# The input projections xr, gr, q and k of a two-layer float32 block, computed with weight columns as the stationary tile

## What is computed

```python
xn = rmsnorm(h, norm_mix_g[l])
u = jnp.einsum('bsd,de->bse', xn, w_in[l])
q, k, v, xr, gr, ga, gb = jnp.split(u, splits, axis=-1)       # 1024 columns each
ya = chunked_band_attention(q, k, v, rel_table[l]) @ w_attn_out[l]
xc = causal_depthwise_conv(xr, conv_w[l], conv_b[l])          # 4 taps along the tokens
hr = rg_lru(xc, w_rg_r[l], b_rg_r[l], w_rg_i[l], b_rg_i[l], rg_lambda[l])
yb = (hr * jax.nn.gelu(gr)) @ w_rnn_out[l]
gates = jax.nn.sigmoid(jnp.concatenate([ga, gb], axis=-1) + b_merge[l])
h = h + (g_a * ya + g_b * yb) @ w_o[l]
```

## Time and profile before

| | us |
|---|---|
| median of 3 runs | 998.67 (997.17 to 1002.05) |
| the profiled execution, its own time | 994.14 |
| its span, first to last instruction | 992.4 |
| PE busy | 952.9 |
| DVE busy | 502.7 |
| ACT busy | 491.2 |
| POOL busy | 337.3 |

### The profile page before, as it was taken

The page is one execution under the profiler, slowest core; times in us unless marked ns, Lnnn a source line. Parts: engine busy times, 40 slices in busy tenths (PEclk is TensorE's granted clock), DMA queues, the critical chain, the costliest instruction groups (busy, mean ns, idle before and its releaser), DMA issues.

```text
span 992.4 us, 13886 instructions
## 1 busy us (share of the span) xinstructions
PE 952.9 (96%) x4548; PEld 786.9 (79%) x4548; DVE 502.7 (51%) x841; ACT 491.2 (49%) x771; POOL 337.3 (34%) x170
## 2 busy tenths in 40 slices
PE   8998979999999999999999999998999989999997
PEld 6876867888878888888878888887878868888886
DVE  5439596554544434343564434337488674334332
ACT  5353935654455454444544454436436464444442
POOL 2410000102434444344444444553512034343442
PEclk9999999999999999999999999999999999999999
DMA  7844454354655566778566566655612246665562
GB/s 232 282 131 147 144 173 141 109 153 142 204 161 181 174 190 190 239 225 242 175 183 190 171 192 188 188 157 161 190 43 86 85 147 194 192 187 175 190 190 81
DMA packets 132768, 169.29 MB, mean 171 GB/s; under 512 B 16707, under 2 KB 88430, under 8 KB 132598
## 3 DMA queue, kind: packets, MB, share of 16 engines
q1 hardware_dynamic: 132566, 168.67, 55.1%
q10 hardware_dynamic: 160, 0.07, 0.0%
HBM read 167.61 MB, written 1.10 MB: 170 GB/s over the span
## 4 chain that ended last, share of the span: by engine, by line
PE 79%; DVE 11%; ACT 5%; issue 3%; DMA 0%; POOL 0%; DVEq 0%; POOLq 0%; ACTq 0%; SPq 0%
PE acc L786 24%; PE acc L788 24%; PE acc L787 24%; PE tp L831 4%; DVE w_lo L1173 4%; ACT w_hi L462 1%; PE sc L916 1%; PE acc L1108 1%; DVE u L1261 1%; ACT junk L468 1%; DVE xt_lo L1556 1%; DVE u L1225 0%; DVE u L1321 0%; DVE h L1546 0%; PE tp L936 0%
## 5 line engine op out<-in xcount | busy, mean ns | idle before, releaser
L462 ACT ACTIVATE w_hi<-w_raw 128x1024 fp32r<-128x1024 f32 x305 | 322.0, 1060 | 376.2 <-PE acc L788 346.0
L1770 POOL TENSOR_TENSOR w_lo<-w_raw,w_hi 128x1024 fp32r<-128x1024 f32 x124 | 302.5, 2440 | 397.0 <-ACT w_hi L462 396.9
L1173 DVE TENSOR_TENSOR w_lo<-w_raw,w_hi 128x1024 fp32r<-128x1024 f32 x181 | 234.8, 1306 | 330.6 <-ACT w_hi L462 328.9
L786 PE MATMUL acc<-w_hi,xt_hi 128*128 128x512 f32 (+1 forms) x880 | 350.0, 398 | 9.5 <-DVE w_lo L1173 6.6
L788 PE MATMUL acc<-w_lo,xt_hi 128*128 128x512 f32 (+1 forms) x880 | 342.9, 390 | 0.0
L787 PE MATMUL acc<-w_hi,xt_lo 128*128 128x512 f32 (+1 forms) x880 | 342.2, 389 | 0.0
L786 PEld LDWEIGHTS acc<-w_hi,xt_hi 128*128 128x128 f32 x880 | 165.3, 188 | 46.6 <-DVE w_lo L1173 9.7
L788 PEld LDWEIGHTS acc<-w_lo,xt_hi 128*128 128x128 f32 x880 | 165.1, 188 | 34.7
L787 PEld LDWEIGHTS acc<-w_hi,xt_lo 128*128 128x128 f32 x880 | 165.5, 188 | 32.0
L786 PE MATMUL acc<-w_hi,hid_hi 128*128 128x512 f32 x264 | 103.2, 391 | 0.0
L788 PE MATMUL acc<-w_lo,hid_hi 128*128 128x512 f32 x264 | 102.8, 389 | 0.0
(11 more groups left out here) (198 smaller groups left out, 781.7 us busy)
## 6 DMA issues: line engine op xcount, KB each, us to landing
w_raw<-in_ffn_w_gu SPq DMA_DIRECT2D x176, 256.0 KB
w_raw<-in_w_in SPq DMA_DIRECT2D x68, 512.0 KB
w_raw<-in_w_ffn_in SPq DMA_DIRECT2D x88, 256.0 KB
w_raw<-in_ffn_w_down SPq DMA_DIRECT2D x44, 512.0 KB
w_raw<-in_w_ffn_out SPq DMA_DIRECT2D x22, 512.0 KB
w_raw<-in_w_rnn_out SPq DMA_DIRECT2D x8, 512.0 KB
w_raw<-in_w_attn_out SPq DMA_DIRECT2D x8, 512.0 KB
w_raw<-in_w_o SPq DMA_DIRECT2D x8, 512.0 KB
```

The costliest lines, as they stand in the source:

```text
L462: act.activation(w_hi[:, b, :], w_raw[:, b, :], ACT.Copy).then_inc(hi_done[b], 1)
L786: pe.matmul(o, hi[:, k, rows], wh, start=first and n == 0, stop=False)
L1173: dve.tensor_tensor(w_lo[:, b, :], w_raw[:, b, :], w_hi[:, b, :].bitcast(F32), ALU.subtract).then_inc(lo_done[b], 1)
L1770: pool.tensor_tensor(w_lo[:, b, :], w_raw[:, b, :], w_hi[:, b, :].bitcast(F32), ALU.subtract).then_inc(lo_done[b], 1)
```

## The change

xr, gr, q and k (groups 0 to 7) are computed turned: a tile of 128 x 128 of the weight is stationary and 256 columns of x transposed stream, so a slab has 24 matmuls of 256 columns in place of 12 of 512, and the result has features on the partitions. The scale rs then lies along the free dimension: DVE spreads it to columns (`rs_cols`), PE turns it once, and DVE keeps it as a row `rx_row`, plain and times 1/8 for q. `evict_turned` multiplies with that row and writes straight to `xrT`, `grT` and `qkT`. The turns of xr, gr, q and k and their copies are gone; gelu works in place on ACT. The parameter turn moves from behind slab 16 to behind slab 4. The convolution moves to slabs 8 to 13 in DVE's queue, the gates to two tiles behind each of slabs 12 to 15 in PE's, with slabs 16 to 19 fed between tanh on ACT. SP loads the block-diagonal weights before slab 8 instead of after slab 15. POOL's queue has the same low halves. The diff, with semaphores and unchanged lines left out:

```diff
-X = starts([("x", 4), ("par", 1), ("xg", 8), ("gate", 8), ("qk", 8), ("p1", 16), ("at", 4), ("mt", 4), ("h1", 4),
+X = starts([("x", 4), ("rs", 1), ("par", 1), ("gate", 8), ("p1", 16), ("at", 4), ("mt", 4), ("h1", 4),
...
+    rs_cols = pt1[:, 1, 0:T].rearrange("p (m t) -> p m t", m=MT)
+    rx_row = sb1[:, :, 0:T]
...
-    rows_k(w_in, 4, 3, 3 * D + W)
+    rows_k(w_in, 4, 1, 3 * D + W)
...
+    with sp.Fori(0, 2) as c:
+        for q in range(4):
+            slab(8 + q, rect(8 + q, w_in, 256 * q, c * W + 4 * D), c, 1)
...
-    with act.Fori(0, 2) as i:
-        feed(4, 8, i, 2)
-    act.wait_ge(set_up, 2)
-    for n in range(4):
-        x = X["xg"] + 2 * n
-        wait_tp_full(act, x)
-        act.activation(xrT[:, 2 * n:2 * n + 2, 3:3 + T],
-                       two(tp[x % 2]), ACT.Copy).then_inc(tp_free[x % 2], 1)
-        x += 1
-        wait_tp_full(act, x)
-        act.activation(grT[:, 2 * n:2 * n + 2, :], two(tp[x % 2]),
-                       ACT.Gelu_apprx_tanh).then_inc(tp_free[x % 2], 1)
+    feed(4, 6)
...
-    feed(20, 11)
+    feed(10, 6)
+    def gelu(g):
+        for b in range(2):
+            wait_drained(act, g, b)
+            v = grT[:, 4 * (g - 2) + 2 * b:4 * (g - 2) + 2 * b + 2, :]
+            act.activation(v, v, ACT.Gelu_apprx_tanh).then_inc(gelu_done, 1)
+    gelu(2)
...
+        if n % 2 == 0:
+            feed(16 + n // 2, 1)
...
+    gelu(3)
...
+        if n % 2 == 0:
+            feed(20 + n // 2, 1)
...
-        if n % 2 and n < 7:
-            feed(31 + n // 2, 1)
-    feed(34, 1)
-    feed(35, 1)
+    feed(24, 4)
...
-    feed(36, 2)
-    for n in range(4):
-        x = X["qk"] + 2 * n
-        wait_tp_full(act, x)
-        act.activation(qkT[:, 2 * n:2 * n + 2, :], two(tp[x % 2]),
-                       ACT.Copy, scale=HD ** -0.5).then_inc(tp_free[x % 2], 1)
-        feed((38, 39, 41, 42)[n], (1, 2, 1, 1)[n])
+    feed(28, 8)
...
-    feed(43, 1)
+    feed(36, 8)
...
+    def group_turned(s, g, ready=None, after={}):
+        banks = acc[g % 2 * 2:g % 2 * 2 + 2]
+        for q in range(4):
+            r = (s + q) % RING
+            pe.wait_ge(lo_done[r], (s + q) // RING + 1)
+            if ready is not None:
+                ready(q)
+            if q == 0:
+                wait_bank(pe, g, 1)
+            for b in range(2):
+                for c in (2 * b, 2 * b + 1):
+                    for j in range(2):
+                        k, cols = 2 * q + j, slice(j * W + c * P, j * W + (c + 1) * P)
+                        o = banks[b][:, c % 2 * T:(c % 2 + 1) * T]
+                        pe.matmul(o, w_hi[:, r, cols], xt_hi[:, k, :], start=q == 0 and c == 2 * b and j == 0,
+                                  stop=False, skip_group_check=True)
+                        pe.matmul(o, w_hi[:, r, cols], xt_lo[:, k, :], start=False, stop=False,
+                                  skip_group_check=True)
+                        mm = pe.matmul(o, w_lo[:, r, cols], xt_hi[:, k, :], start=False, stop=q == 3 and j == 1,
+                                       skip_group_check=True)
+                if b == 0 and q == 3:
+                    mm.then_inc(acc0_full[g % 2], 1)
+                if b == 1:
+                    mm.then_inc(slab_used[r], 1)
+            if q in after:
+                after[q]()
...
-    group(0, 0, XT, 4, ready=pairs_ready(X["x"]), after={0: lambda: turn_x(2), 1: lambda: turn_x(3)})
-    for g in range(1, 4):
-        group(4 * g, g, XT, 4)
-    def turn_xr_gr(tile_pairs):
-        for g in range(4):
-            wait_both_drained(pe, g)
-        for n in tile_pairs:
-            turn_tiles(X["xg"] + 2 * n, u[:, 0], (2 * n, 2 * n + 1))
-            turn_tiles(X["xg"] + 2 * n + 1, u[:, 1], (2 * n, 2 * n + 1))
-    def turn_parameters():
+    def turn_rs_and_parameters():
+        pe.wait_ge(rs_spread, 1)
+        turn(X["rs"], [(m * P, rs_cols[:, m, :]) for m in range(MT)])
...
-        turn_xr_gr((0, 1))
-    group(16, 4, XT, 4, after={0: turn_parameters, 1: lambda: turn_xr_gr((2, 3))})
-    group(20, 5, XT, 4)
-    def gates():
+    def gates(n0):
...
-        for n in range(KT):
+        for n in (n0, n0 + 1):
...
-    def turn_q_k(n):
-        for sec in (2, 3):
-            wait_both_drained(pe, 2 * sec + n // 2)
-            turn_tiles(X["qk"] + 2 * n + sec - 2, u[:, sec], (2 * n, 2 * n + 1))
-    group(24, 6, XT, 4, after={2: gates})
-    group(28, 7, XT, 4)
-    group(32, 8, XT, 4, after={1: lambda: turn_q_k(0), 2: lambda: turn_q_k(1)})
-    group(36, 9, XT, 4, after={0: lambda: turn_q_k(2), 1: lambda: turn_q_k(3)})
-    wait_tp_free(pe, X["qk"] + 6)
-    wait_tp_free(pe, X["qk"] + 7)
+    group_turned(0, 0, ready=pairs_ready(X["x"]), after={0: lambda: turn_x(2), 1: lambda: turn_x(3)})
+    group_turned(4, 1, after={0: turn_rs_and_parameters})
+    group_turned(8, 2)
+    group_turned(12, 3, after={q: lambda q=q: gates(2 * q) for q in range(4)})
+    for g in range(4, 8):
+        group_turned(4 * g, g)
+    group(32, 8, XT, 4)
+    group(36, 9, XT, 4)
+    wait_both_drained(pe, 6)
+    wait_both_drained(pe, 7)
...
-    with dve.Fori(0, 2) as i:
-        for g in range(2):
-            feed(4 + 4 * g, 4, i, 2)
-            drain_scaled(g, lambda m: u[:, bass.ds(i, 1), m, g * W:(g + 1) * W].rearrange("p a n -> p (a n)"),
-                         i, 2, 1, 4 * g + 3, rx)
+    dve.tensor_copy(rs_cols, rx.unsqueeze(2).to_broadcast([P, MT, P])).then_inc(rs_spread, 1)
+    feed(4, 4)
+    wait_tp_full(dve, X["rs"])
+    step(dve.tensor_copy(rx_row[:, 0, :], tp[X["rs"] % 2][:, 0:T]))
+    dve.tensor_scalar(rx_row[:, 1, :], tp[X["rs"] % 2][:, 0:T], HD ** -0.5, None,
+                      ALU.mult).then_inc(tp_free[X["rs"] % 2], 1)
...
+    def evict_turned(g, dst, row=0):
+        for b in range(2):
+            wait_acc(dve, g, b, 4 * g + 3)
+            tiles = slice(4 * (g % 2) + 2 * b, 4 * (g % 2) + 2 * b + 2)
+            dve.tensor_tensor(dst(tiles), two(acc[g % 2 * 2 + b]),
+                              rx_row[:, row, :].unsqueeze(1).to_broadcast([P, 2, T]),
+                              ALU.mult).then_inc(acc_drained[g % 2 * 2 + b], 1)
+    def to_xr(tiles):
+        return xrT[:, tiles, 3:3 + T]
+    wait_tp_free(dve, X["rs"])
+    evict_turned(0, to_xr)
...
-    wait_tp_free(dve, X["xg"] + 6)
-    wait_tp_free(dve, X["xg"] + 7)
...
-    feed(20, 2)
+    wait_both_drained(dve, 0)
...
-    feed(22, 2)
+    feed(8, 2)
...
-    drain_section(4)
-    feed(24, 2)
+    evict_turned(1, to_xr)
+    feed(10, 2)
+    wait_both_drained(dve, 1)
+    conv_tiles((4, 5))
+    feed(12, 2)
+    conv_tiles((6, 7))
...
-    conv_tiles((4, 5))
-    feed(26, 2)
-    conv_tiles((6, 7))
-    drain_section(5)
-    dve.wait_ge(table_landed, 16)
-    dve.tensor_copy(ext_sb[:, 256:384], ext_sb[:, 255:256].to_broadcast([HEADS, P])).then_inc(ext_done, 1)
-    feed(28, 4)
-    drain_section(6)
-    feed(32, 2)
+    evict_turned(2, lambda tiles: grT[:, tiles, :])
+    feed(14, 4)
+    evict_turned(3, lambda tiles: grT[:, tiles, :])
+    feed(18, 4)
+    wait_tp_free(dve, X["gate"] + 6)
+    wait_tp_free(dve, X["gate"] + 7)
+    dve.wait_ge(conv_done, KT)
+    step(dve.scalar_tensor_tensor(ti[:], ti[:], 1.0, xcT, ALU.add, ALU.mult))
+    feed(22, 1)
+    evict_turned(4, lambda tiles: qkT[:, tiles, :], 1)
+    feed(23, 2)
...
+    feed(25, 1)
...
-    feed(34, 2)
-    wait_tp_free(dve, X["gate"] + 6)
-    wait_tp_free(dve, X["gate"] + 7)
-    step(dve.scalar_tensor_tensor(ti[:], ti[:], 1.0, xcT, ALU.add, ALU.mult))
-    drain_section(7)
-    def copy_k(n):
-        x = X["qk"] + 2 * n + 1
-        wait_tp_full(dve, x)
-        dve.tensor_copy(qkT[:, KT + 2 * n:KT + 2 * n + 2, :], two(tp[x % 2])).then_inc(tp_free[x % 2], 1)
+    feed(26, 1)
+    evict_turned(5, lambda tiles: qkT[:, tiles, :], 1)
+    feed(27, 2)
+    dve.wait_ge(table_landed, 16)
+    dve.tensor_copy(ext_sb[:, 256:384], ext_sb[:, 255:256].to_broadcast([HEADS, P])).then_inc(ext_done, 1)
+    dve.wait_ge(mult_done, 1)
+    dve.scalar_tensor_tensor(ti[:], ti[:], 0.5, sq, ALU.mult, ALU.mult).then_inc(bx_done, 1)
+    feed(29, 1)
...
-    feed(36, 2)
-    copy_k(0)
-    dve.wait_ge(mult_done, 1)
-    dve.scalar_tensor_tensor(ti[:], ti[:], 0.5, sq, ALU.mult, ALU.mult).then_inc(bx_done, 1)
...
-    feed(38, 2)
-    copy_k(1)
+    feed(30, 1)
+    def to_k(tiles):
+        return qkT[:, slice(KT + tiles.start, KT + tiles.stop), :]
+    evict_turned(6, to_k)
...
-    drain_section(8)
-    feed(40, 2)
-    copy_k(2)
-    copy_k(3)
+    feed(31, 2)
...
+    dve.wait_ge(gelu_done, 4)
...
-    feed(42, 2)
-    drain_section(9)
+    feed(33, 2)
+    evict_turned(7, to_k)
+    feed(35, 2)
...
+    def drain_section(g):
+        drain_scaled(g, lambda m: u[:, g // 2, m, g % 2 * W:(g % 2 + 1) * W], last_slab=4 * g + 3, scale=rx)
+    feed(37, 2)
+    drain_section(8)
+    feed(39, 4)
+    drain_section(9)
+    feed(43, 1)
...
-    with pool.Fori(0, 2) as i:
-        feed(4, 8, i, 2)
+    feed(4, 16)
...
-    wait_tp_free(pool, X["qk"])
```

(7 more changed lines are left out.)

## The result

The changed kernel takes 985.1 us (median of 4 runs, 983.9 to 987.3) beside 998.9 for the kernel before (median of 4 runs, 997.2 to 1002.1): a ratio of 0.9866, 95% interval 0.9847 to 0.9885. It is faster by 13.8 us. The forecast was 992.5, 6.2 us faster: right in sign and inside its range, but 7.4 us above what was measured. The profiled execution has a time of 987.3 and a span of 985.5 us at a mean granted clock of 0.994.

What follows compares the result with a forecast made beforehand. PE's queue was taken as the bound (busy 96% of the span). First scores 3.8 us earlier plus 2.4 from the first attention round made 6.2 us, so 998.7 became 992.5; range 982 to 1001 over all cases.

Steps and rivals of the forecast that it cites:

- the time of the first scores: Start of the first attention scores on PE: 145.1 us instead of 148.9, 3.8 us of the gain.
- the DVE chain: DVE's queue from 26.2 us through convolution, polynomial and group 2's eviction: through at 60.1, with 9.2 us for POOL meetings.
- ACT between the eviction and the third gate tile: ACT's gelu 0.6, high half 1.06, table load 1.28 and tanh 0.9 us: third gate tile starts about 64.0.
- the last of the sum: Final step: median 998.7, 4.5 above the profiled execution, and the same 6.2 us off gives 992.5.
- Clock, before: PE's waits in the kernel before, the longest half of 6 us: granted clock stays at 1.00, 2.4 GHz, through all.
- Turned slabs: PE, 24 matmuls of 256 columns per slab, 0.1192 us each with hidden weight loads: 2.86 us, 0.13 more than now.
- Rival 2: PE's turned slabs: weight loads aren't hidden; gate-pass spacing of 0.22 us would add 42 us, giving 1035; chance 0.06.
- Rival 4: Supply of slabs, not PE, sets the pace; 10 us of waits come back elsewhere: no change, 998; chance 0.06.
- rival 1: DVE and POOL don't get in each other's way: scores at 134.0, 17.3 us less, 981.4; chance 0.18.
- Clock, after: PE after its new 6 us idle before the third gate tile: clock may fall to 1.2 GHz, costing 1.9 us.
- rival 3: Clock stays low between PE's stops from 64 to 76 us: +9.6 over the forecast, 1002; chance 0.10.
- First round: First attention round, 20.58 us: PE's wait for the first softmax goes as yt_lo moves earlier, 2.4 us less.

Runs made afterwards that it cites:

- a_again: The changed kernel run once more with no edit, beside the kernel before: median 986.1 us (6 runs), ratio 0.9879.
- b_again: The kernel before, run once more with no edit: median 997.8 us (12 runs), ratio 1.0006; its profiled execution took 997.75 us.
- b_split: The kernel before with matmuls of slabs 0 to 31 cut in two of 256 columns, x still stationary: 1001.35 us, ratio 1.0031.
- a_lo_dve: The changed kernel with the low halves of slabs 9 to 19 that POOL made now made by DVE: 980.2 us, ratio 0.9818.
- a_fill: The changed kernel with nine unused matmuls filling PE's idle before the third gate tile: 984.2 us, ratio 0.9857.
- a_yt_late: The changed kernel with yt_lo put back behind the low half of slab 43, just ahead of the first maxima: 986.5 us, ratio 0.9883.

## Why the prediction was right and wrong, point by point

**Two steps failed.** The first is the time of the first scores. The sum has them at 145.1; a_again, with an ordinary start, has them at 141.6, 3.5 us earlier. Three terms on the way were too large, by 1.5 us (the DVE chain), 1.5 (ACT between the eviction and the third gate tile) and 1.0 (the gates), and the slabs were 0.4 too small; the points below take them one by one.

The second is the last of the sum: "the median of the runs shown is 998.7, 4.5 above the profiled one, and the same 6.2 off gives 992.5". It takes the 4.5 us for something that both kernels share. b_again shows what such a difference is made of, falls of the clock after waits of PE, 1.6 us of them at the very wait that the change removes. a_again has 1.6 us of such falls, the one at 264 us, besides the one that the sum counts for itself. So 2.9 of the 4.5 us were too much.

Both together close the sum for a_again: 992.5 - 3.5 - 2.9 = 986.1, as measured. The first result, 985.1, lies 1.0 lower; the intervals of the two ratios overlap, and no run says more about that. From the sum's own base the forecast was 987.9, and the profiled execution after took 987.3; that agreement is luck. Its scores came 2.1 us early (3.5, less 1.4 for a late transfer of x and a fall of the clock behind it), and a fall at 268 us that the sum didn't have took 1.6 back.

Between two executions that have their falls, b_again and a_again, the gain is 7.3 us up to the first scores (148.89 to 141.61), 2.4 in the first round and 1.6 for the fall at the softmax wait; then b_again loses 2.0 us to two more falls and a_again 1.6 to one. That is all of the 11.7 us between them. The forecast had 3.8, 2.4 and 0.

**Clock, before.** "through all those the granted clock stays at 1.00" held for one execution and was read as a property of the kernel. That it stood 4.5 us under the median was the hint that it wasn't.

**Turned slabs: right.** The timeline of PE and of weight loads in the kernel after, inside a turned slab (compare):

```profile
99.70 0.28 PE L840 MATMUL acc<-xt_lo,w_hi 128*128 128x256 f32 x1
99.82 0.28 PE L842 MATMUL acc<-xt_hi,w_lo 128*128 128x256 f32 x1
...
99.70 0.19 PEld L842 LDWEIGHTS acc<-xt_hi,w_lo 128*128 128x128 f32 x1
99.82 0.19 PEld L838 LDWEIGHTS acc<-xt_hi,w_hi 128*128 128x128 f32 x1
```

Starts are 0.12 us apart with a load of 0.19 us for each: 24 matmuls in 2.86 to 2.87 us, and 24 slabs in 68.05 us for 67.6 forecast. Rival 2 is out, and b_split prices the form by itself. The Trainium skill (TensorE: Matmul & The Clock Gate, "What overlaps and what doesn't") lets a weight load overlap a running matmul only in another row group; in this trace both use all 128 rows and overlap throughout, so the measurement decides against it here. Rival 4 is out as well: no gap before slabs 16 to 39.

**The DVE chain: right in kind, 1.5 us too long.** Forecast from 26.2 to 60.1, 33.9 us; measured 27.6 to 60.0, 32.4. The four meetings cost 2.07, 2.17, 2.07 and 2.15 us (the groups above less their times in a_lo_dve), 8.5 together for 9.2; the five small operations took 0.5 us for 0.9. `consts_ready` came at 58.8, as forecast, from a start that was 1.4 us late. The first pair of convolution tiles met nothing: it was POOL that waited there. POOL in the kernel after:

```profile
32.58 4.29 POOL L1802 TENSOR_TENSOR w_lo<-w_raw,w_hi 128x1024 fp32r<-128x1024 f32 x1 [2.71 <-ACT w_hi L469]
37.64 2.40 POOL L1802 TENSOR_TENSOR w_lo<-w_raw,w_hi 128x1024 fp32r<-128x1024 f32 x1 [0.76 <-ACT w_hi L469]
...
51.53 4.20 POOL L1802 TENSOR_TENSOR w_lo<-w_raw,w_hi 128x1024 fp32r<-128x1024 f32 x1 [5.04 <-ACT w_hi L469]
```

4.29 us for an operation that takes 2.40. So slab 8 was not late (1.5 forecast), slab 10 came 2.3 us late and slab 12 0.4. Two turned evictions took 1.28 us for 1.33, undisturbed in the middle of POOL's work. As a forecast for the change rival 1 is refuted by the chain above. That its 981.4 lay nearer to the result than 992.5 comes from the steps named at the start, of which 0.7 us at most have to do with POOL (8.5 for 9.2). a_lo_dve builds the case without meetings: its first scores are at 134.86, near the rival's 134.0, though 6.8 us before a_again's and not the 11.1 that the rival put between its own and the forecast's.

**ACT before the gates: one term was not there.** ACT in the kernel after:

```profile
51.47 1.28 ACT L512 ACT_TABLE_LOAD   x1
59.45 1.23 ACT L512 ACTIVATE grT<-grT 128x512 f32<-128x512 f32 x2 [6.69 <-DVE grT L1255]
60.58 1.04 ACT L469 ACTIVATE w_hi<-w_raw 128x1024 fp32r<-128x1024 f32 x1
61.53 0.46 ACT L521 ACTIVATE u<-tp,small 128x256 f32<-128x256 f32 x1
...
79.34 1.28 ACT L532 ACT_TABLE_LOAD   x1
```

The load stands ahead of gelu, in ACT's idle time, and none stands between gelu and tanh. The forecast had put 1.28 us between them, the duration of the earlier trace rows, where a load stands before another operation. Without it, 2.5 us passed from the eviction to the third gate tile for 4.0. The tile came at 62.49 instead of 64.1, and the idle was 4.2 us for 6.

**Clock, after: right in kind.** After the idle the first gate passes of the kernel after run long:

```profile
63.57 1.06 PE L903 MATMUL tp<-u,blockdiag 128*128 128x256 f32 x2
64.42 1.06 PE L904 MATMUL tp<-u,blockdiag 128*128 128x256 f32 x2
64.92 0.78 PE L838 MATMUL acc<-xt_hi,w_hi 128*128 128x256 f32 x1
65.49 0.41 PE L840 MATMUL acc<-xt_lo,w_hi 128*128 128x256 f32 x1
65.70 0.41 PE L842 MATMUL acc<-xt_hi,w_lo 128*128 128x256 f32 x1
```

Matmuls of 256 columns start 0.21 us apart, the 1.2 GHz level again, for 0.12. It cost 1.7 us (a_fill) for 1.9 forecast. It didn't stay low between stops, so rival 3 is out. What the forecast lacked is that shorter waits do the same: at 266.96, after 1.91 us behind DVE (L1455), the next matmuls of 512 columns are 0.43 apart too, 1.6 us.

**Gates with slabs 14 and 15**: 10.7 us without the fall for 11.5, so the restarts were priced 0.8 too high. **First round**: 18.19 us, 2.4 less, as forecast, and the maxima start 2.5 us behind the scores for 2.6. `yt_lo` is not all of it (a_yt_late). **Start**: slab 4 at 24.3 for 22.7 in the profiled execution and 22.9 in a_again, so the forecast stands and the first trace had a late transfer of x. In sum for the first scores: start +1.4, chain -1.5, ACT -1.5, gates -1.0, slabs +0.4 make 142.9 out of 145.1; measured 142.97. In a_again the start is 0, and the same terms make 141.5; measured 141.61.

## What to carry to other kernels

Price an edit against an execution that looks like the median: where the profiled one lies several us under it, its waits are cheaper than usual, and a wait of 2 us that goes may take as much again in clock with it. When operations move on DVE, look at what POOL runs at that time; here four meetings of 2.1 us each were worth more than sharing the low halves with POOL, and moving them off POOL, with one activation put behind the ones that PE waits for, gave 8 to 9 us more than the change alone.

## What the runs showed of the hardware that was not expected

- A DVE operation with a single tensor operand, SBUF to SBUF, is held by POOL's as well: 53.43 us, 128x8 elements, 2.33 us instead of 0.18. The Trainium skill (GPSIMD Engine Reference, "Key points") names two SBUF inputs or a 2-port mode as the condition; no run here shows which mode this one was in. Evictions out of PSUM were not held: two in 1.28 us at 28.69 while POOL worked from 23.71 to 29.87. The holding goes both ways, 4.29 us on POOL for 2.40.
- A fall of the clock to 1.2 GHz after a wait of PE of only some 2 us (1.65 at 157.49 in b_again, 1.91 at 266.96 after), in some executions and not in others: the kernel before's first trace has the same 1.65 us at 157.52 and no fall. One costs 0.8 to 1.7 us, and three of them are the 3.6 us between two executions of the same kernel.
- gelu and tanh are served without a table load between them, while the load at 79.34, before the operation at L532, is 1.28 us.
